# Prompt attention items: normalised probabilities, and a value product that comes out turned

## The reference

```python
logits = jnp.einsum('bthgd,btnhd->bthgn', qg, k_sel).astype(jnp.float32) * (HEAD_DIM ** -0.5)
logits = jnp.where(sel_ok[:, :, None, None, :], logits, -jnp.inf)
prob = jax.nn.softmax(logits, axis=-1).astype(v_sel.dtype)
o = jnp.einsum('bthgn,btnhd->bthgd', prob, v_sel)
return o.reshape(B, Tq, N_HEADS * HEAD_DIM)      # then o @ w_out
```

## Time and profile before

| | |
|---|---|
| time, median of 3 runs | 3695.96 us (3693.06 to 3700.19) |
| profiled execution, own time | 3719.19 us |
| its span (first to last instruction) | 3717.4 us |
| mean granted TensorE clock | 0.979 of full |
| PE busy in the span | 3545.0 us (95%), 21469 matmuls |
| DVE, ACT, POOL busy | 67%, 37%, 50% |
| chain that ended last, by engine | PE 68%, DVE 17%, DMA 6%, issue 4% |

### The profile page before, as it was taken

How to read it: one execution, slowest core, us unless ns; L and a number is a source line. 1 busy time by engine, 2 the same in 40 slices (tenths; PEclk the granted TensorE clock), 3 DMA queues, 4 the chain that set the end, 5 groups by cost and what they waited for, 6 DMA issues and landing times.

```text
span 3717.4 us, 62204 instructions
## 1 busy us (share of the span) xinstructions
PE 3545.0 (95%) x21469; PEld 3389.2 (91%) x21469; DVE 2487.7 (67%) x5354; ACT 1364.9 (37%) x1921; POOL 1849.4 (50%) x1170
## 2 busy tenths in 40 slices
PE   7999999999999999999888789999999999999998
PEld 7999999999999999999873469999999999999998
DVE  3342597778775777776578533679696866778783
ACT  3322343535443333333221353344444443333332
POOL 3434466555655555552551324456555655556551
PEclk9999999999999999999999799999999999999999
DMA  3222367877878999994335422467777889999992
GB/s 131 80 69 91 103 190 244 282 243 266 271 281 271 313 305 319 313 327 138 86 113 172 130 66 91 135 196 248 275 235 278 276 282 278 296 319 307 320 307 97
DMA packets 392485, 812.75 MB, mean 219 GB/s; under 512 B 52008, under 2 KB 249576, under 8 KB 384888
## 3 DMA queue, kind: packets, MB, share of 16 engines
q1 hardware_dynamic: 172032, 459.92, 37.0%
q0 software_dynamic: 64176, 229.53, 18.1%
q10 hardware_dynamic: 156048, 120.37, 11.0%
HBM read 696.96 MB, written 112.74 MB: 218 GB/s over the span
## 4 chain that ended last, share of the span: by engine, by line
PE 68%; DVE 17%; DMA 6%; issue 4%; POOL 2%; ACT 2%; SPq 0%; another core or an unknown queue 0%; ACTq 0%; DVEq 0%; POOLq 0%
PE acc L629 42%; PE acc L616 15%; DMA rows<-u_in,expertP 4%; PE misc L765 3%; DVE rows L1831 3%; DMA raw<-slabs_in 2%; POOL w_lo L2265 1%; DVE misc L1766 1%; PE misc L1041 1%; DVE route L1770 1%; DVE hot_gate L1869 1%; PE misc L805 1%; ACT w_hi L1102 1%; DVE idxs L2111 1%; DVE passed L2099 1%
## 5 line engine op out<-in xcount | busy, mean ns | idle before, releaser
L2265 POOL TENSOR_TENSOR w_lo<-raw,w_hi 128x1024 fp32r<-128x1024 f32 x368 | 901.7, 2451 | 1042.6 <-ACT w_hi L1102 1041.3
L629 PE MATMUL acc<-h_hi,w_hi 128*128 128x416 f32 x3072 | 1097.1, 357 | 2.3 <-DVE x L1977 1.4
L629 PE MATMUL acc<-h_lo,w_hi 128*128 128x416 f32 x3072 | 1085.0, 353 | 0.0
L629 PE MATMUL acc<-h_hi,w_lo 128*128 128x416 f32 x3072 | 1080.6, 352 | 0.0
L1102 ACT ACTIVATE w_hi<-raw 128x1024 fp32r<-128x1024 f32 x620 | 656.6, 1060 | 1116.8 <-DMA raw<-slabs_in 1074.9
L629 PEld LDWEIGHTS acc<-h_hi,w_hi 128*128 128x128 f32 x3072 | 580.5, 189 | 10.8 <-POOL h_lo L2307 1.3
L629 PEld LDWEIGHTS acc<-h_hi,w_lo 128*128 128x128 f32 x3072 | 581.1, 189 | 7.1
L629 PEld LDWEIGHTS acc<-h_lo,w_hi 128*128 128x128 f32 x3072 | 580.7, 189 | 3.7
L1948 DVE TENSOR_TENSOR w_lo<-raw,w_hi 128x1024 fp32r<-128x1024 f32 x252 | 332.7, 1320 | 211.5 <-ACT w_hi L1102 211.3
L1831 DVE CUSTOM_DVE_ANT_0 rows<-acc,rows 128x1024 f32<-128x1024 f32 (+1 forms) x224 | 273.6, 1222 | 202.6 <-DMA rows<-u_in,expertP 182.2
L629 PE MATMUL acc<-y_hi,w_hi 128*128 128x416 f32 x1024 | 363.3, 355 | 11.4 <-POOL y_lo L2307 6.6
(11 more groups left out here) (349 smaller groups left out, 5650.0 us busy)
## 6 DMA issues: line engine op xcount, KB each, us to landing
raw<-slabs_in SPq DMA_DIRECT2D x620, 512.0 KB
act_d<-gelu SPq DMA_DIRECT2D x256, 208.0 KB
gate_d<-gout SPq DMA_DIRECT2D x52, 1024.0 KB
abuf<-act_d ACTq DMA_DIRECT2D x32, 1664.0 KB, 12.3
gbuf<-gate_d ACTq DMA_DIRECT2D x30, 1664.0 KB
unit<-ck_in SPq DMA_DIRECT2D x72, 128.0 KB, 2.3
vquad<-cv_in SPq DMA_DIRECT2D x64, 128.0 KB
unit<-ck_in ACTq DMA_DIRECT2D x56, 128.0 KB, 2.5
```

Source lines behind the costliest of these rows:

```text
L629: last = pe.matmul(acc[:, 0, par, 0:ND], w[:, c, :], m(c), start=c == 0 and w is w_hi[r] and m is m_hi, stop=c == KC - 1 and w is w_lo[r])
L2265: pool.tensor_tensor(w_lo[r][:], raw[r][:], w_hi[r][:].bitcast(F32), ALU.subtract).then_inc(lo_done, 1)
```

## The change

- `output` is gone. A new DVE step `normal(i)`, two iterations behind `biased`, takes the reciprocal of one row sum and multiplies the whole probability tile `prob[i % 5]` (128 (b+1) columns) in place. `turn(i)` now waits for this step instead of for the exponential.
- `pv` works on a head pair p (items 2p and 2p+1) at odd i. The values are the stationary side (64 columns), the turned probabilities move (128 columns each), and the two heads' outputs go to the two halves of the array's columns, so the result has the head dimension on its partitions: it comes out turned. `probT` gets four slots instead of two.
- `block_output` is gone with its transposes. Instead ACT `out_high(p)` and DVE `out_low(p)` split each pair's 128x128 result into `h_hi` and `h_lo`.
- Nothing else in the program differs. The tile `o_tok` and the semaphores `o_done` and `oT_done` go, `norm_done` comes.

```diff
--- before.py
+++ after.py
@@ -305,9 +305,8 @@
         again_take = region(t_at)
         prob = [again_take(f"prob{r}", [P, 512]) for r in range(2)]
         prob += [at(f"prob{2 + r}", [P, 512], F32, qi_at + r * 2048) for r in range(3)]
-        probT = [again_take(f"probT{r}", [P, 4, P]) for r in range(2)]
-        qM = at("qM", [P, 2, TS * (P + 16)], F32, again_take.end)
-        o_tok = again_take("o_tok", [P, D])
+        probT = [again_take(f"probT{r}", [P, 4, P]) for r in range(4)]
+        qM = at("qM", [P, 2, TS * (P + 16)], F32, again_take.end - 4096)
         oS_tok = at("oS_tok", [P, 4 * P], F32, qi_at + 3 * 2048)
         pT_s = again_take("pT_s", [P, PAGES, P])
         take = region(max(after_tiles, again_take.end))
@@ -423,7 +422,7 @@
         s_log_taken = sem("s_log_taken")
         log_done, log_taken = sem("log_done"), sem("log_taken")
         exp_done, ptr_done, pT_done, pv_done = sem("exp_done"), sem("ptr_done"), sem("pT_done"), sem("pv_done")
-        o_done, oT_done, oT_hi, oT_lo = sem("o_done"), sem("oT_done"), sem("oT_hi"), sem("oT_lo")
+        norm_done, oT_hi, oT_lo = sem("norm_done"), sem("oT_hi"), sem("oT_lo")
         hit_ready, behind_loaded = sem("hit_ready"), sem("behind_loaded")
         digit_done = sem("digit_done")
         s_max_done, s_exp_done, s_prob_done = sem("s_max_done"), sem("s_exp_done"), sem("s_prob_done")
@@ -1020,42 +1019,30 @@
 
                 def turn(i):
                     b, h = divmod(i, NHEAD)
-                    pe.wait_ge(exp_done, i + 1)
+                    pe.wait_ge(norm_done, i + 1)
                     if i >= 2:
                         pe.wait_ge(pT_done, i - 1)
-                    if b and h in (1, 2):
-
-                        pe.wait_ge(oT_lo, 2 * b)
                     for k in range(b + 1):
                         last = pe.transpose(acc[:, 1, i % 2, k * P:(k + 1) * P], prob[i % 5][:, k * P:(k + 1) * P],
                                             ident[:])
                     last.then_inc(ptr_done, 1)
 
-                def pv(i):
-                    b, h = divmod(i, NHEAD)
-                    pe.wait_ge(pT_done, i + 1)
-                    if i >= 2:
-
-                        pe.wait_ge(o_done, i - 1)
+                def pv(p):
+
+                    b, c = divmod(p, NHEAD // 2)
+                    pe.wait_ge(pT_done, 2 * p + 2)
+                    if p >= 2:
+
+                        pe.wait_ge(oT_lo, p - 1)
                     for k in range(b + 1):
-                        last = pe.matmul(misc[:, i % 2, 0:HD], probT[i % 2][:, k, :],
-                                         v_tok[:, k, (h // 4) * HD:(h // 4 + 1) * HD], start=k == 0, stop=k == b)
+                        for odd in range(2):
+                            last = pe.matmul(misc[odd * HD:(odd + 1) * HD, p % 2, 0:P],
+                                             v_tok[:, k, (c // 2) * HD:(c // 2 + 1) * HD],
+                                             probT[(2 * p + odd) % 4][:, k, :], start=k == 0, stop=k == b)
                     last.then_inc(pv_done, 1)
-
-                def block_output(b):
-
-                    pe.wait_ge(o_done, NHEAD * (b + 1))
-                    pe.wait_ge(pT_done, min(NHEAD * (b + 1) + 1, ITEMS))
-                    for k in range(8):
-                        last = pe.transpose(acc[:, 1, k // 4, (k % 4) * P:(k % 4 + 1) * P], o_tok[:, k * P:(k + 1) * P],
-                                            ident[:])
-                        if k % 4 == 3:
-                            last.then_inc(oT_done, 1)
 
                 pe.wait_ge(s_pT_done, NU + 1)
                 for i in range(ITEMS + 5):
-                    if i >= NHEAD + 4 and (i - 4) % NHEAD == 0:
-                        block_output((i - 4) // NHEAD - 1)
                     if i % 2 == 0 and i < ITEMS:
                         if i >= 2:
                             pe.wait_ge(log_taken, i - 1)
@@ -1063,8 +1050,8 @@
                         log_of(i + 1)
                     if 3 <= i < ITEMS + 3:
                         turn(i - 3)
-                    if 4 <= i < ITEMS + 4:
-                        pv(i - 4)
+                    if i % 2 and i >= 5:
+                        pv((i - 5) // 2)
                     if i % 4 == 3 and i < ITEMS:
                         s_values(i // 4)
 
@@ -1072,7 +1059,7 @@
                 for c in range(4):
                     last = pe.transpose(misc[:, 3, c * P:(c + 1) * P], oS_tok[:, c * P:(c + 1) * P], ident[:])
                 last.then_inc(oS_turned, 1)
-                pe.wait_ge(oT_lo, 8)
+                pe.wait_ge(oT_lo, ITEMS // 2)
                 pe.wait_ge(oS_done, 2)
 
             linear("q0", 1)
@@ -1499,19 +1486,19 @@
                 def take_turned(i):
                     b = i // NHEAD
                     act.wait_ge(ptr_done, i + 1)
-                    if i >= 2:
-                        act.wait_ge(pv_done, i - 1)
-                    act.activation(probT[i % 2][:, 0:b + 1, :], acc[:, 1, i % 2, 0:(b + 1) * P].rearrange(
+                    if i >= 4:
+                        act.wait_ge(pv_done, i // 2 - 1)
+                    act.activation(probT[i % 4][:, 0:b + 1, :], acc[:, 1, i % 2, 0:(b + 1) * P].rearrange(
                         "p (k t) -> p k t", t=P), ACT.Copy).then_inc(pT_done, 1)
 
-                for i in range(ITEMS + 5):
-                    if i >= NHEAD + 4 and (i - 4) % NHEAD == 0:
-                        b = (i - 4) // NHEAD - 1
-                        for k in range(2):
-                            act.wait_ge(oT_done, 2 * b + k + 1)
-                            act.activation(h_hi[:, 4 * k:4 * k + 4, b * P:(b + 1) * P],
-                                           acc[:, 1, k, :].rearrange("p (k t) -> p k t", t=P), ACT.Copy).then_inc(
-                                oT_hi, 1)
+                def out_high(p):
+                    b, c = divmod(p, NHEAD // 2)
+                    act.wait_ge(pv_done, p + 1)
+                    act.activation(h_hi[:, c, b * P:(b + 1) * P], misc[:, p % 2, 0:P], ACT.Copy).then_inc(oT_hi, 1)
+
+                for i in range(ITEMS + 6):
+                    if i % 2 == 0 and i >= 6:
+                        out_high((i - 6) // 2)
                     if 3 <= i < ITEMS + 3:
                         take_turned(i - 3)
                     if i < ITEMS:
@@ -2205,32 +2192,27 @@
                                              scale=-(HD ** -0.5), scalar=-LOW, op0=ALU.add, op1=ALU.min,
                                              accum_out=nmx[:, i:i + 1]).then_inc(log_taken, 1)
 
-                def output(i):
-                    b, h = divmod(i, NHEAD)
-                    if b and h == 0:
-
-                        dve.wait_ge(oT_done, 2 * b)
-                    if i % 2 == 0:
-                        dve.wait_ge(exp_done, i + 2)
-                        dve.reciprocal(rinv[:, i:i + 2], psums[:, i:i + 2]).then_inc(dve_step, step.up())
-                        dve.wait_ge(dve_step, step.at)
-                    dve.wait_ge(pv_done, i + 1)
-                    dve.tensor_scalar(o_tok[:, h * HD:(h + 1) * HD], misc[:, i % 2, 0:HD],
-                                      rinv[:, i:i + 1], None, ALU.mult).then_inc(o_done, 1)
-
-                for i in range(ITEMS + 5):
-                    if i >= NHEAD + 4 and (i - 4) % NHEAD == 0:
-                        b = (i - 4) // NHEAD - 1
-                        for k in range(2):
-                            dve.wait_ge(oT_hi, 2 * b + k + 1)
-                            part = h_hi[:, 4 * k:4 * k + 4, b * P:(b + 1) * P]
-                            dve.tensor_tensor(h_lo[:, 4 * k:4 * k + 4, b * P:(b + 1) * P],
-                                              acc[:, 1, k, :].rearrange("p (k t) -> p k t", t=P), part.bitcast(F32),
-                                              ALU.subtract).then_inc(oT_lo, 1)
+                def normal(i):
+                    n = (i // NHEAD + 1) * P
+                    dve.wait_ge(exp_done, i + 1)
+                    dve.reciprocal(rinv[:, i:i + 1], psums[:, i:i + 1]).then_inc(dve_step, step.up())
+                    dve.wait_ge(dve_step, step.at)
+                    dve.tensor_scalar(prob[i % 5][:, 0:n], prob[i % 5][:, 0:n], rinv[:, i:i + 1], None,
+                                      ALU.mult).then_inc(norm_done, 1)
+
+                def out_low(p):
+                    b, c = divmod(p, NHEAD // 2)
+                    dve.wait_ge(oT_hi, p + 1)
+                    dve.tensor_tensor(h_lo[:, c, b * P:(b + 1) * P], misc[:, p % 2, 0:P],
+                                      h_hi[:, c, b * P:(b + 1) * P].bitcast(F32), ALU.subtract).then_inc(oT_lo, 1)
+
+                for i in range(ITEMS + 6):
+                    if i % 2 and i >= 7:
+                        out_low((i - 7) // 2)
                     if i < ITEMS:
                         biased(i)
-                    if 4 <= i < ITEMS + 4:
-                        output(i - 4)
+                    if 2 <= i < ITEMS + 2:
```

(1 more changed line is left out.)

## The result

The changed kernel takes 3708.4 us (median of 14 runs, 3698.8 to 3728.5) against 3696.9 us of the kernel before (14 runs, 3685.0 to 3703.1). The ratio is 1.0036, with a 95% interval of 1.0025 to 1.0048: 9 to 18 us slower. The forecast was 3704.4 us, just slower, so the direction was right and the loss of 8.4 us somewhat low.

The account below looks back on a forecast made before the run. PE was taken as the bound, busy for 95% of the span. The terms 13.6 - 6.9 - 1.8 + 1.0 + 2.5 gave +8.4 us, on 3696.0 a forecast of 3704.4 us, range 3684 to 3719.

Parts of the forecast that it names:

- Step 1: Value product on PE: priced like a pair's scores, 0.49, 0.70, 0.91, 1.12 us in blocks 0 to 3, 0.06 overlapping.
- Steps 2 and 3: Each prompt pair's second turn waits behind scores, `biased` and `normal`; pairs take 1.93 to 4.11 us, +13.6 us in all.
- the gaps cost clock and stops in full: Rival, blocks 0 to 2: more time at 1.2 GHz (5 to 7 us), stops 5.5 us more; 3716 us, chance 0.17.
- Step 4: Three block ends: eight transposes each and PE's 3.8 us wait for `h_lo` go, -6.9 us.
- Step 5: Tail after the last scores: eight transposes and two ACT copies go, one smaller copy comes, -1.8 us.
- Step 7: Blocks 0 to 2: DVE's scalings slowed beside POOL's DMA issues, +1.0 us.
- DVE is locked out: Rival, blocks 0 to 2: each scaling beside a POOL issue pays a whole issue, 0.95 us; 3713 us, chance 0.05.
- Step 8: Blocks 0 to 2: stalled hand-overs between engines, costing PE 8.9 us before, hit the closed chain harder, +2.5 us.
- The rivals on the other side: Clock holds in blocks 0 to 2: 3692 us, 0.14; wait covered by PE's idle time: 3690 or 3683 us, 0.14.

Follow-up runs that it names:

- pv_serial: norm_first with the value product's loops exchanged: all key tiles of the even head, then the odd head's, instead of alternating; ratio 0.9979 to the kernel before.
- norm_first: The changed kernel with `normal(i-2)` ahead of `biased(i)` in DVE's order; 3683.9 us, ratio 0.9968 to the kernel before.

## Why the prediction came out as it did

- *Step 1, the new product like the scores.* Right. Forecast 1.06 us in block 3 up to what follows; from its start at 2176.20 to the next scores at 2177.22 it is 1.02. Both halves run side by side, and pv_serial's 1.58 us shows that the alternating order makes them.
- *Steps 2 and 3, the closed chain.* Right to 0.01 us: 4.12, 3.38 and 2.64 us, forecast 4.11, 3.38 and 2.65. The delay of the second turn's load, 2.51 us after the scores, was forecast as 2.51. Three runs bear the cause out: taking the chain away (norm_first) saves 17 to 24 us of the stage, lengthening it by 0.32 us costs a pair 0.33, and adding it alone to the kernel before costs 7 us. Only the base of block 2 was off: I took the middle of its neighbours, 2.95, where the pair before takes 2.89.
- *Block 0: the chain right, the clock missing.* At the same clock the change costs a pair 0.42 or 0.43 us, where 0.45 was forecast: at 1.2 GHz 2.61 us against 2.19, and 4.48 against 4.05 with the samples' step; at 2.4 GHz 2.91 against 2.48 with that step. (The one plain pair wholly at 2.4 GHz took 2.05 us, forecast 1.93, with a scaling on its path that took 0.14 longer than its kind.) But the sum had no term for how much of the block runs at 1.2 GHz. By the mean clocks, 0.72 before and 0.55 and 0.84 after, that was 10 us in the second profile of the kernel before, and 23 and 7 us in the two of the changed kernel. So block 0 took 6.9 us more in the one and 2.3 in the other, where the term was 3.6, and block 1 of the first, at 0.91, took another 2.2. This is a part of the rival "the gaps cost clock and stops in full", priced on all three blocks; it came true in block 0 and a little in block 1 of the first profile, and not in the second. Whether the longer gaps hold the clock down isn't settled: the kernels with the full chain had 0.55, 0.56 and 0.84 in block 0, the one with the scaling alone 0.91, the others 0.71 to 1.00, and with one or two executions each these overlap.
- *Step 4, the block ends.* Too large: I took 3.8 us for `h_lo` from the profile with stops; undisturbed it is 2.5. The term is -5.6, not -6.9.
- *Step 5, the tail.* 10.2 us instead of 11.9: -1.7, forecast -1.8.
- *Step 7, DVE beside POOL.* Nearly right, and small. The scalings by form in the changed kernel:

```profile
L2200 DVE TENSOR_SCALAR prob<-prob,rinv 128x512 f32<-128x512 f32 x16 | 8.0, 501 | 0.6
L2200 DVE TENSOR_SCALAR prob<-prob,rinv 128x384 f32<-128x384 f32 x16 | 6.8, 424 | 0.6
L2200 DVE TENSOR_SCALAR prob<-prob,rinv 128x256 f32<-128x256 f32 x16 | 6.1, 383 | 0.6
L2200 DVE TENSOR_SCALAR prob<-prob,rinv 128x128 f32<-128x128 f32 x16 | 5.1, 318 | 0.6
```

  Against 486, 420, 353 and the shortest, 286, they are 15, 4, 30 and 32 ns longer in the mean, 1.3 us over all 64, half of which lie on the path: 0.6 us against 1.0. All of it lies beside POOL: in this profile the 28 scalings that overlap none of POOL's DMA issues took their usual time, and the other 36 were 0.035 us longer in the mean and 0.21 at most (the longest took 702 ns).

  My reading of the earlier trace rows was wrong here. The five casts of line 1726 that took 596 to 1621 ns weren't long for a DMA issue: they stood beside a `tensor_tensor` of POOL of 2.4 us (one at 485.20 to 487.61 us, the cast at 486.16 to 487.78) and ended 0.15 to 0.16 us after it, while the three with nothing of POOL beside them took 289 to 291. The rival "DVE is locked out" rested on these casts. The Trainium skill ("SBUF — State Buffer", "Who interferes with whom") says that the loser of the lock is blocked until the other's instruction is through. The five casts agree with it; the scalings lose far less than a DMA issue of 0.95 us.
- *Step 8, the stops,* was wrong in kind. I read the 8.9 us as a cost of every execution and let the change pay 2.5 us more. The nine other profiles have none, neither before nor after. The hint was in the text: the profiled execution lay 23.2 us over the median, and I put that down to reasons outside this stage, when it was this stage. Since the sum was made of differences, the harm stayed small: 2.5 us too many for the stops, and 1.3 us too many taken off at the block ends, which pull in opposite directions. Against the 1.2 us that remain stands the clock, for which there was no term and which moved blocks 0 and 1 by -1.3 us in one profile and +5.5 in the other. That the total came so near is in part luck.
- *The rivals on the other side* failed where they were to decide: the wait wasn't covered (31 waits of PE, 0.67 us each); and the clock had nothing to give back in blocks 1 and 2, which stood at 1.00 in the second profile of the kernel before, and didn't hold in block 0.

With the terms as measured, 2.5 + 3.9 + 4.1 us for blocks 3 to 1 (7, 8 and 8 pairs at 0.35, 0.49 and 0.51), 6.9 for block 0 and 2.2 for the clock of block 1, -5.6, -1.7 and 0.6, the sum is 12.9 us for the first profile; with 2.3 for block 0 and nothing for block 1 it is 6.1 for the second. Their stages give 13.8 and 7.0, and the timed runs 9 to 18 and 6 to 13.

## What to carry to other kernels

Cheaper work on the busiest engine brought nothing here, because the same edit put another engine's step between two of its own steps in the same iteration. Write the two in-order lists side by side and ask, for each wait, which of the waiter's own recent instructions the awaited one stands behind. Here the cure was the order within DVE's list, and after it the place of the product in PE's. And when the profiled execution is dearer than the median by more than the effect in question, find where it is dearer before taking any term of a sum from it; a second profile is the cheapest experiment. And compare stretches at the same granted clock: block 0 of one and the same program took 20.7 us and 25.3.

## What wasn't expected of the hardware

One profiled execution of the kernel before had stops in which ACT and DVE resumed together after up to 2.3 us, and a stage of 137.1 us; another of the same program had 112.0 and none. The cause of the stops stays open; none of the nine other profiles shows one. Column halves addressed in runs instead of alternately still overlapped, for four of eight matmuls: 1.58 us for sixteen matmuls of 128 columns, 1.09 when alternating. And DVE casts that began beside a `tensor_tensor` of POOL ended only 0.15 to 0.16 us after it, while DVE's scalings lost 0.21 us at most to POOL's DMA issues of 0.95.
